# Removing the 65 matmuls that write an unread PSUM bank inside the five normalisations of a Trainium2 kernel

## The reference, cut to what matters

```python
def layer_norm(x, g, b):
    mu = jnp.mean(xf, -1, keepdims=True)
    var = jnp.mean(jnp.square(xf - mu), -1, keepdims=True)
    return ((xf - mu) * lax.rsqrt(var + LN_EPS) * g + b).astype(x.dtype)
...
x = layer_norm(ALPHA * x + mix, ln_mix_g[i], ln_mix_b[i])
x = layer_norm(ALPHA * x + conv_ffn(...), ln_ffn_g[i], ln_ffn_b[i])
```

## Time and profile before

| | |
|---|---|
| time, median of 3 runs | 2629.14 us |
| lowest and highest of them | 2625.03 and 2636.7 us |
| the profiled execution's own time | 2629.51 us |
| its span in the profile | 2627.7 us |
| granted TensorE clock, mean over the span | 0.989 of full |
| PE busy | 2535.7 us (96%) |
| DVE, ACT, POOL busy | 1373.9, 982.4, 188.0 us |

### The profile page before, as it was taken

The page is one execution under the profiler, slowest core; times in us unless marked ns, Lnnn a source line. Parts: engine busy times, 40 slices in busy tenths (PEclk is TensorE's granted clock), DMA queues, the critical chain, the costliest instruction groups (busy, mean ns, idle before and its releaser), DMA issues. The chain is left out here.

```text
span 2627.7 us, 34010 instructions
## 1 busy us (share of the span) xinstructions
PE 2535.7 (96%) x12200; PEld 1979.4 (75%) x12200; DVE 1373.9 (52%) x1975; ACT 982.4 (37%) x1727; POOL 188.0 (7%) x338
## 2 busy tenths in 40 slices
PE   8999999999999999999999899899998999999999
PEld 7777776888786876688878587678886667778777
DVE  6655426777324344577742567745555654542532
ACT  4333424333213254433321334624344652431331
POOL 0000001000001022100000100300101540000000
PEclk9999999999999999999999999999999999999999
DMA  4222222333222320233322132042222003323232
GB/s 128 82 72 72 81 90 70 96 96 96 90 93 62 90 65 17 64 97 98 98 91 96 45 97 89 1 138 78 73 81 57 1 1 96 89 89 95 80 96 96
DMA packets 277343, 206.62 MB, mean 79 GB/s; under 512 B 12100, under 2 KB 233969, under 8 KB 277233
## 3 DMA queue, kind: packets, MB, share of 16 engines
q1 hardware_dynamic: 270465, 198.64, 25.7%
q10 hardware_dynamic: 6768, 6.51, 0.8%
HBM read 203.02 MB, written 2.10 MB: 78 GB/s over the span
## 5 line engine op out<-in xcount | busy, mean ns | idle before, releaser
L150 DVE TENSOR_TENSOR WL<-RAW,WH 128x1024 fp32r<-128x1024 f32 x362 | 443.5, 1225 | 876.7 <-ACT WH L145 870.6
L145 ACT ACTIVATE WH<-RAW 128x1024 fp32r<-128x1024 f32 x362 | 383.1, 1058 | 1134.5 <-PE PS L159 876.5
L157 PE MATMUL PS<-XH,WH 128*128 128x512 f32 x1568 | 619.8, 395 | 10.9 <-DVE LT L2779 4.0
L158 PE MATMUL PS<-XL,WH 128*128 128x512 f32 x1568 | 612.6, 391 | 0.0
L159 PE MATMUL PS<-XH,WL 128*128 128x512 f32 x1568 | 612.5, 391 | 0.0
L157 PEld LDWEIGHTS PS<-XH,WH 128*128 128x128 f32 x1568 | 296.0, 189 | 77.5 <-issue 10.9
L159 PEld LDWEIGHTS PS<-XH,WL 128*128 128x128 f32 x1568 | 295.7, 189 | 62.9
L158 PEld LDWEIGHTS PS<-XL,WH 128*128 128x128 f32 x1568 | 296.1, 189 | 60.7 <-issue 1.0
L154 PE MATMUL PS<-WH,XH 128*128 128x512 f32 x416 | 164.6, 396 | 4.6 <-DVE CPOS L2547 2.7
L156 PE MATMUL PS<-WL,XH 128*128 128x512 f32 x416 | 162.7, 391 | 0.0
L155 PE MATMUL PS<-WH,XL 128*128 128x512 f32 x416 | 162.6, 391 | 0.0
(11 more groups left out here) (503 smaller groups left out, 3701.8 us busy)
## 6 DMA issues: line engine op xcount, KB each, us to landing
RAW<-in_ffn_w_up SPq DMA_DIRECT2D x88, 512.0 KB, 3.8
RAW<-in_w_in SPq DMA_DIRECT2D x60, 512.0 KB, 3.6
RAW<-in_ffn_w_down SPq DMA_DIRECT2D x44, 512.0 KB, 3.6
RAW<-in_sc_ssm_w_in SPq DMA_DIRECT2D x42, 512.0 KB, 3.8
RAW<-in_w_mlp_up SPq DMA_DIRECT2D x32, 512.0 KB, 4.0
RAW<-in_w_mlp_down SPq DMA_DIRECT2D x32, 512.0 KB, 3.7
RAW<-in_fox_w_in SPq DMA_DIRECT2D x24, 512.0 KB, 3.8
RAW<-in_sc_ssm_w_out SPq DMA_DIRECT2D x16, 512.0 KB, 3.7
```

The lines of the kernel that those rows point to most:

```text
L145: act.activation(WH[:, slot, :], RAW[:, slot, :], ACT.Copy).then_inc(hi_ready, 1)
L150: dve.tensor_tensor(WL[:, slot, :], RAW[:, slot, :], WH[:, slot, :], ALU.subtract).then_inc(lo_ready, 1)
L157: pe.matmul(o, wh, ah, start=first, stop=False)
L158: pe.matmul(o, wh, al, start=False, stop=False)
```

## The change

Both calls of `fill_pe` in `ssq_pe` go, and the helper with them. Nothing else differs.

```diff
-    def fill_pe(pe, n):
-        for _ in range(n):
-            pe.matmul(PS[:, 5, :], WH[:, 0, 0:P], WH[:, 0, 512:1024], start=True, stop=True)
-
     def ln_pe(pe, s):
...
             last = pe.matmul(PS[:, 6, c:c + 1], LT[:, 2, c * P:(c + 1) * P], ONES[:, 0:1], start=True, stop=True)
         last.then_inc(s.var, 1)
-        fill_pe(pe, 5)
         pe.wait_ge(s.dg, s.at.dg + 1)
         pe.matmul(PS[:, 7, :], ONES[:, :], LT[:, 4, :], start=True, stop=True).then_inc(s.bc, 1)
-        fill_pe(pe, 8)
```

## The result

Without the filling matmuls the kernel takes 2646.74 us at the median of 10 runs (2645.29 to 2647.64), against 2632.3 (2625.03 to 2637.73) for 10 runs of the kernel before. The ratio is 1.0059, with a 95% interval of 1.0047 to 1.0070: slower by 0.6%, inside the range of the prediction (2628 to 2648) and 8.7 us above its 2638. Of these 8.7 us, 2.8 lie in the starting point, for the prediction started from 2629.5 and ten runs have 2632.3; the loss itself is 14.4 us where 8.75 were forecast. The profiled execution took 2646.95 us, 17.4 more than that of before (2629.51), which lay 2.8 us under the median of its kernel.

A forecast was written before the change was run, and what follows sets the result against it. PE was taken to bound the kernel. Norms 1 to 3 at 2.45 us each, norm 5 at 0.9 and norm 4 at 0.5 sum to 8.75 us, added to 2629.5 for 2638 us; range 2628 to 2648.

The forecast's parts named there:

- PE sets the time, and removed filling matmuls are off the path: Whole kernel: PE busy 2535.7 of 2627.7 us; removal saves nothing at full clock, except 0.8 us in norm 5.
- The clock falls at every norm: Idle 1.33 and 3.02 us around each norm's spread was expected to bring TensorE's clock down to 0.5.
- 2.45 us for each of norms 1 to 3, 7.35 together: Per norm: 11 dense matmuls at half rate, 2.2 us, plus one chance in three of a slow spread, 0.25 us.
- Norm 5, 0.9 us: Slow dense matmuls behind norm 5, 2.2 us, less 0.5 absorbed and 0.8 from a spread no longer held up.
- Norm 4, 0.5 us: Norm 4 and norm 5's sums: slow spread 0.25 us, last group of sums at 0.5 another 0.25 us.
- Faster, same or slower: Whole time against 0.5%, 13.1 us: faster 0.03, the same 0.74, slower 0.23.
- The likeliest case: Whole kernel: clock falls as priced, 8.75 us slower, 2638 us, own range 2633 to 2643; chance 0.62.
- the dearest falls: Upper bound over all five norms: 10.8 us for norms 1 to 3, 2.8 norm 5, 1.6 norm 4; 15.2 us.
- The second rival: At the norms: the spread mid-lull keeps the clock up; only norm 5's 0.8 us shows, 2628.7 us; chance 0.12.
- The third: All five norms: filling delays the spread, removal gains 4 us, 2625.5 us; chance 0.09 shared with loss taken back later.
- The first rival: Clock at 0.5 from before the spread into dense work: 3.6 us at norms 1 to 3, 2.8 at norm 5; chance 0.17.
- The mean clock: Over the profiled span, the mean granted clock was to fall from 0.989 by about 0.005.

The follow-up runs named there:

- Narrow filling: All 65 filling matmuls kept in place but passing 32 columns instead of 512, against the kernel before: 2645.85 us, ratio 1.0050.
- Four buffers: The kernel without filling matmuls, with norm 5 squaring into four LT tiles instead of three: 2635.69 us, ratio 1.0019 against the kernel before.
- More filling: The kernel before plus eight filling matmuls ahead of the sums of norms 1 to 4 and three between norm 5's groups: 2625.68 us, ratio 0.9988.

## Why the prediction was right, and what was mis-sized

*PE sets the time, and removed filling matmuls are off the path.* Right. 65 matmuls less gave no time back, except in norm 5.

*The clock falls at every norm.* Right, with the idle 1.33 and 3.01 us as worked out. Its evidence was thinner than that, as waits of 2.04 us had gone both ways, and the prediction gave a fall 0.62 + 0.17. Narrow filling shows it for cause and not only for company: the same instructions at the same places, less through the array, and the loss is there in full.

*2.45 us for each of norms 1 to 3, 7.35 together.* The profile has 3.25, 2.75 and 2.73, 8.7 together. Without the scatter at the sums ahead (0.13, 1.01 and -0.18) it is 3.12, 1.74 and 2.91, 7.8 together, so the sum was right. Its two terms were less so. The dense matmuls cost 2.18, 1.58 and 1.96 us where 2.2 was taken: 11, 8 and 10 of them ran at half rate, and 0.20 us each is confirmed. The spread was slow in two of the three (and in norms 4 and 5, 2.07 or 2.08 us, against 1.29 in norm 2), where one in three was taken; that cost 0.94, 0.16 and 0.95 us for 0.25.

*Norm 5, 0.9 us.* Taken out alone its own parts read 0.7 in the profile, and nothing that can be measured in the time. The give-and-take of the slow dense matmuls and the spread that is freed was the right one; but the spread was there to be freed only because the trace of before had fallen in norm 5, and an execution whose clock stays up there loses 2.7. After the whole change it is 1.9, because the clock is then low from norm 4 on and little is freed.

*Norm 4, 0.5 us.* This is the step that failed: "a slow spread in one of three cases (0.25) and a last group of sums at 0.5 in as many". It took the squares' sums for work that only its last group could delay. Taken out alone norm 4 costs 4.95 us, and with norm 5 7.3, against 1.4 in the sum. After the change norm 4's two parts are 0.95 for the spread and 3.58 for all four groups, 4.5 us in place of 0.5. The trace of before had the row that would have told it: ACT waits 0.72 us for PE between two squares (1485.00), though another such wait is put down to POOL. A chain that goes to and fro between two engines over too few buffers has every slow step of either on it. Four buffers took 5.8 of the 7.3 us away, 4.2 of them in these sums.

*Faster, same or slower.* The likeliest case was a loss within 0.5%, with a chance of 0.74; the measured one is 0.59%, which had 0.23. With 7.3 in the place of 1.4 the sum would have been 14.6 us, 2644. With the parts as measured, 7.8 for norms 1 to 3, 4.5 for norm 4 and 1.9 for norm 5, it is 14.2, beside the 14.4 by which the medians differ. The measured 2646.7 lies above the 2644.7 that the prediction worked out for the dearest falls, and within the range only because some of the runs' spread was added to it; the loss itself, 14.4 us, stays under the 15.2 of that bound. The second rival, a clock that the spread keeps up, didn't occur: two waits of 1.33 and 3.01 us with the spread between them brought the clock down at every norm. The third, norms held up by filling, is seen in norm 5 alone. The first rival came nearest to the total (2643 to 2645). Its fall, from before the spread until well into the dense matmuls, is what norms 1, 3 and 5 show; but its price there, 3.6 us, was too high, and it too had no long fall through norm 5's sums. The mean clock fell by 0.012 where 0.005 was forecast, for the same reason.

The Trainium skill's rule that activity releases the throttle (TensorE: Matmul & The Clock Gate, Part 1) agrees with every run here that bears on it. No run contradicts it, and narrow filling shows that matmuls alone are not yet activity: 13 of 32 columns in each norm kept nothing up.

What stays open is the scatter, and with it how near the single traces are to the usual execution. Waits of one length in the same code are followed by a fall in one execution and not in another, so that the runs of before spread over 12.7 us. No run here controlled it. The 1.5 us that the profile lost away from the norms is put down to it, but apart from the one place named above that is argued and not shown.

## What to carry to other kernels

Work that nobody reads can be worth its place: before removing (or adding) filler on TensorE, read the granted clock in the stretches behind each lull, and price a fall as the matmuls that start at half rate, 0.20 us each for 512 columns. Put filler where the longest idle time ends in dense work, here behind the spread, and make it as wide as the matmuls that kept the clock here, 512 columns. And ask what else runs on a slow TensorE: a chain that passes few buffers between PE and another engine loses at every step, and its gaps can keep the clock low. Read more than one execution before pricing a place: the trace of before had 3 us of falls in norms 4 and 5 that others did not.

## What the runs showed of the hardware that was not expected

- Once the clock is at 0.5, work with gaps need not bring it back. With norm 4 empty it stayed there for 23.7 us, through norm 4's lull and all of norm 5's sums with 0.79 us between groups, and came back once filling matmuls ran without a gap. It also came back while the same sums ran without gaps (four buffers, 6.07 us).
- Eight matmuls of 32 columns at 0.5 show as 2.51 us of busy time, and don't hold the clock.
- The kernel whose clock falls at every norm has the steadier time: 10 runs within 2.4 us (2645.29 to 2647.64), against 12.7 us for the kernel before. More filling, whose clock falls at no norm, is steadier too (4.3 us over 11 runs). But no filling with four buffers falls at every norm and spreads over 9.1 us, so a fall at every norm is not enough for a steady time.
